# Summing the second conditioning product beside the mixers, in plain fp32

## The reference

```
cond = silu(c)                                   # c is one row of 1024
for l in range(2):
    mod = cond @ w_ada[l] + b_ada[l]             # w_ada[l]: 1024 x 6144
    sh1, sc1, g1, sh2, sc2, g2 = split(mod, 6)
    h = rms_norm(x, g_norm_mix[l]) * (1 + sc1) + sh1
    z = h @ w_in[l]                              # 1024 x 2884
    mix = concat(sparse_attention(z), gated_recurrence(z), spatial_gating(z)) @ w_out[l]
    x = x + g1 * mix
    h = rms_norm(x, g_norm_ffn[l]) * (1 + sc2) + sh2
    y = swiglu(h) if l == 0 else mixture_of_8_experts(h)
    x = x + g2 * y
x = rms_norm(x, g_final)
```

## Time and profile before

| | us |
|---|---|
| median of 3 runs | 2792.98 (2789.38 to 2796.92) |
| the profiled execution | 2798.46 |
| its span | 2796.6 |
| PE busy | 2393.7 |
| DVE busy | 1965.3 |
| ACT busy | 1401.6 |
| mean granted clock of TensorE | 0.897 of full |

### The profile page before, as it was taken

The page is one execution under the profiler, slowest core; times in us unless marked ns, Lnnn a source line. Parts: engine busy times, 40 slices in busy tenths (PEclk is TensorE's granted clock), DMA queues, the critical chain, the costliest instruction groups (busy, mean ns, idle before and its releaser), DMA issues.

```text
span 2796.6 us, 31058 instructions
## 1 busy us (share of the span) xinstructions
PE 2393.7 (86%) x12719; PEld 2029.0 (73%) x12719; DVE 1965.3 (70%) x2326; ACT 1401.6 (50%) x1354; POOL 28.0 (1%) x52
## 2 busy tenths in 40 slices
PE   5836899886378799999999999998758898878898
PEld 4726699865266688888888888886647898746898
DVE  6565654476446588888888888887554787675787
ACT  5322443342423477777776777776324434365432
POOL 1000000000000000000000000000000000000000
PEclk9866999988568799999999999999867999878999
DMA  9410745563004699999999999998421455321453
GB/s 334 134 45 5 270 150 182 200 226 124 6 19 166 233 355 357 354 355 354 356 345 348 357 354 356 355 356 307 124 75 55 147 184 195 97 76 55 145 187 106
DMA packets 293717, 590.70 MB, mean 211 GB/s; under 512 B 11702, under 2 KB 86564, under 8 KB 292928
## 3 DMA queue, kind: packets, MB, share of 16 engines
q1 hardware_dynamic: 289872, 572.33, 58.0%
q0 software_dynamic: 3696, 16.32, 1.9%
HBM read 587.56 MB, written 1.05 MB: 210 GB/s over the span
## 4 chain that ended last, share of the span: by engine, by line
PE 59%; DVE 4%; ACT 2%; DMA 1%; issue 1%; DVEq 0%; POOL 0%; SPq 0%; ACTq 0%
PE ps L1129 18%; PE ps L1131 17%; PE ps L1130 17%; PE ps L1213 1%; PE ps L1337 1%; PE ps L1198 1%; PE ps L1320 1%; PE ps L1298 1%; ACT arena L892 1%; DVE arena L1815 1%; PE ps L1236 1%; DVE arena L1650 1%; DVE xT_lo L1682 0%; DVE w_lo L1635 0%; PE ps L1187 0%
## 5 line engine op out<-in xcount | busy, mean ns | idle before, releaser
L792 ACT ACTIVATE w_hi<-raw 128x2048 fp32r<-128x2048 f32 x548 | 1041.9, 1907 | 610.5 <-PE ps L1131 486.0
L1635 DVE TENSOR_TENSOR w_lo<-raw,w_hi 128x2048 fp32r<-128x2048 f32 x548 | 1224.8, 2273 | 56.1 <-ACT w_hi L792 37.1
L1129 PE MATMUL ps<-w_hi,xT_hi 128*128 128x512 f32 (+3 forms) x1600 | 641.6, 401 | 56.3 <-DVE xT_lo L1749 25.3
L1130 PE MATMUL ps<-w_lo,xT_hi 128*128 128x512 f32 (+3 forms) x1600 | 627.7, 392 | 0.0
L1131 PE MATMUL ps<-w_hi,xT_lo 128*128 128x512 f32 (+3 forms) x1600 | 627.3, 392 | 0.0
L1129 PEld LDWEIGHTS ps<-w_hi,xT_hi 128*128 128x128 f32 x1600 | 310.1, 194 | 124.7 <-DVE xT_lo L1749 26.6
L1130 PEld LDWEIGHTS ps<-w_lo,xT_hi 128*128 128x128 f32 x1600 | 310.4, 194 | 62.6 <-issue 3.4
L1131 PEld LDWEIGHTS ps<-w_hi,xT_lo 128*128 128x128 f32 x1600 | 309.6, 194 | 63.2
L1129 PE MATMUL ps<-xT_hi,w_hi 128*128 128x256 f32 x1056 | 302.4, 286 | 6.0 <-DVE xT_lo L1682 6.0
L1130 PE MATMUL ps<-xT_lo,w_hi 128*128 128x256 f32 x1056 | 301.8, 286 | 0.0
L1131 PE MATMUL ps<-xT_hi,w_lo 128*128 128x256 f32 x1056 | 301.7, 286 | 0.0
(11 more groups left out here) (324 smaller groups left out, 1916.3 us busy)
## 6 DMA issues: line engine op xcount, KB each, us to landing
raw<-in_moe_w_gate SPq DMA_DIRECT2D x112, 1024.0 KB, 5.5
raw<-in_moe_w_up SPq DMA_DIRECT2D x112, 1024.0 KB, 5.3
raw<-in_moe_w_down SPq DMA_DIRECT2D x112, 1024.0 KB, 5.4
raw<-in_w_ada SPq DMA_DIRECT2D x48, 1024.0 KB, 5.3
raw<-in_f_w_up SPq DMA_DIRECT2D x44, 1024.0 KB, 5.0
raw<-in_f_w_down SPq DMA_DIRECT2D x22, 1024.0 KB, 4.9
raw<-in_w_in SPq DMA_DIRECT2D x20, 1024.0 KB, 5.1
raw<-in_a_w_in SPq DMA_DIRECT2D x12, 1024.0 KB, 5.4
```

The lines of the kernel that those rows point to most:

```text
L792: act.activation(w_hi[:, k % HI, 0:LEN[k]], raw[:, r, 0:LEN[k]], ACT.Copy).then_inc(w_hi_ready, 1)
L1129: pe.matmul(out_, lh, rh, start=start, stop=False)
L1130: pe.matmul(out_, lh, rl, start=False, stop=False)
L1635: dve.tensor_tensor(w_lo[:, k % RAW, 0:LEN[k]], raw[:, k % RAW, 0:LEN[k]], w_hi[:, k % HI, 0:LEN[k]].bitcast(F32), ALU.subtract).then_inc( ...
```

## The change

- `ada{l}1` moves in `ORDER` ahead of `out{l}`, and its 12 slots (`WHOLE`) are not split: ACT and DVE skip them, and PE multiplies them as loaded in plain fp32 with a stationary fp32 vector `cond_wide` (`whole`, new). The 12 slots are used in four places of PE's mixer program: slots 0 to 2 ahead of the transposes of the heads, 3 to 7 after the index scores, 8 and 9 ahead of the recurrence, 10 and 11 after its output. They use PSUM banks 4 to 7; ACT copies the six sums out (`whole_sums`, new).
- The bias of this half goes to its own place (`bias_late`); bias and sums are added between the two groups of `out{l}` (shift and scale) and after the norm rows (gate).
- In `ada{l}0` the squares, the root and the norm rows are computed between groups 2 and 3 and after group 3, beside the two gate groups, and the transposed rows go to banks 4 to 7.
- The angles of both position sets are computed in `in0`, after groups 1 and 3. At the start the vector `c` and the identity are loaded first, then the bias, `x`, the gain, and the other constants.
- The first two slots of `out{l}` are split during the two root waits of the mixer's end. `h_LF` moves from `arena` to `mix`.
- The norm gains of the second half, of `g_final` and of `kv_norm` are released (and so loaded) right after the preceding norm's rows; the root is taken ahead of the wait for the gain.

```diff
-        h_LF = Cut(arena)(768, b=2)
+        h_LF = mix[:, :, 0:BD]
+        bias_late = arena[:, 8448:8448 + 3 * D]
-        ORDER = ["ada00", "in0", "out0", "ada01", "ffn0", "ada10", "in1", "out1", "ada11", "over", "moe",
+        ORDER = ["ada00", "in0", "ada01", "out0", "ffn0", "ada10", "in1", "ada11", "out1", "over", "moe",
+        WHOLE = [BASE[name] + i for name in ("ada01", "ada11") for i in range(len(SL[name]))]
+        WHOLE_BANKS = [4, 5, 6, 7, 4, 4]
...
 # POOL
-            load(const[:, :], consts, ld_const)
+            load(cond_rows, a["c"][0].rearrange("(k p) -> k p", p=P), ld_cond)
+            load(ident, consts[:, C_ID:C_ID + P], ld_ident)
+            load(arena[:, 0:3 * D], a["b_ada"][0, 0:3 * D].partition_broadcast(P), ld_mod)
             load(X[:, :, :], a["x"][0].rearrange("(b p) n -> p b n", p=P), ld_x)
-            load(cond_rows, a["c"][0].rearrange("(k p) -> k p", p=P), ld_first)
+            load(gain, a["g_norm_mix"][0].partition_broadcast(P), ld_gain)
+            load(const[:, P:C_END], consts[:, P:C_END], ld_const)
...
 # ACT
+            def conditioned(name):
+                upto(BASE[name] + 6)
+                square_sums(X)
+                upto(BASE[name] + 7)
+                root(rstd)
+                linear(name)
+                to_columns(bank=4)
+            def whole_sums(l, groups):
+                for g in groups:
+                    act.wait_ge(w_used, BASE[f"ada{l}1"] + 2 * g + 2)
+                    dst = gate_sums[:, 512 * g - 2048:512 * g - 1536] if g >= 4 else arena[:, 512 * g:512 * g + 512]
+                    act.activation(dst, ps[:, WHOLE_BANKS[g], :], ACT.Copy).then_inc(ada_sums, 1)
...
+                upto(BASE[f"out{l}"])
                 act.wait_ge(o_out, got(o_out))
...
+                whole_sums(l, [5])
+                upto(BASE[f"out{l}"] + 1)
                 root(stat_b[:, 0:2])
                 to_columns(3)
                 linear(f"out{l}")
-                cond_columns()
-                linear(f"ada{l}1")
...
 # PE
+            def whole(l, slots):
+                for i in slots:
+                    k = n[0]
+                    pe.wait_ge(raw_full[k % RAW], 16 * (k // RAW + 1))
+                    n[0] += 1
+                    for c in range(4):
+                        last = pe.matmul(ps[:, WHOLE_BANKS[i // 2], :], cond_wide[:, i % 2 * 4 + c, :],
+                                         raw[:, k % RAW, c * FG:(c + 1) * FG], start=i % 2 == 0 and c == 0,
+                                         stop=i % 2 == 1 and c == 3)
+                    last.then_inc(w_used, 1)
...
                 linear(f"in{l}")
+                pe.wait_ge(cond_wide_ready, l + 1)
+                whole(l, range(0, 3))
                 pe.wait_ge(heads_ready, got(heads_ready))
...
+                whole(l, range(3, 8))
                 pe.wait_ge(idx_taken, got(idx_taken))
+                pe.wait_ge(ada_sums, got(ada_sums, 4))
                 attend(dsa[l], att_bufs, att_T, [
...
+                whole(l, range(8, 10))
                 pe.wait_ge(rec_rows, got(rec_rows))
...
                 last.then_inc(o_out, 1)
+                pe.wait_ge(ada_sums, got(ada_sums))
+                whole(l, range(10, 12))
                 pe.wait_ge(ws_masked, got(ws_masked))
...
                 linear(f"out{l}")
-                pe.wait_ge(cond_cols, got(cond_cols))
-                linear(f"ada{l}1", 1, True)
+                got(ada_sums)
                 to_columns(H)
...
 # DVE, in ada()
+                def rows_of_norm():
+                    upto(BASE[name] + len(SL[name]) - 1)
+                    scale_with_gain()
+                    norm_rows(True)
+                between = {2: inv_rms, 3: rows_of_norm}
+                if name == "ada00":
+                    between[1] = rows_in_memory
+                linear(name, evac, between, 1)
+                to_columns(bank=4)
...
+                linear(f"in{l}", into_rows(zrows(IN_DIM)), {} if l else {1: first_angles, 3: second_angles})
...
-                inv_root(stat_a[:, 0:12], stat_a[:, 0:12], HD)
+                inv_root(stat_a[:, 0:12], stat_a[:, 0:12], HD, lambda: upto(BASE[f"out{l}"]))
...
-                inv_root(stat_b[:, 0:2], stat_b[:, 0:2], C_DIM)
+                inv_root(stat_b[:, 0:2], stat_b[:, 0:2], C_DIM, lambda: upto(BASE[f"out{l}"] + 1))
...
-                linear(f"out{l}", into_residual(True))
-                beat().then_inc(mod_free, 1)
-                dve.wait_ge(mod_free, sent(mod_free))
-                ada(f"ada{l}1")
-                norm(True)
+                def shift_and_scale():
+                    mods[0] += 16
+                    dve.wait_ge(ld_mod, mods[0])
+                    dve.wait_ge(ada_sums, 6 * l + 4)
+                    tt(arena[:, 0:2 * D], arena[:, 0:2 * D], bias_late[:, 0:2 * D], ALU.add)
+                    scale_with_gain()
+                linear(f"out{l}", into_residual(True), {0: shift_and_scale})
+                inv_rms()
+                norm_rows(True)
+                gain_taken()
+                dve.wait_ge(ada_sums, 6 * l + 6)
+                tt(mod[:, 2, :], gate_sums[:, :], bias_late[:, 2 * D:3 * D], ALU.add)
+                to_columns()
```

More of the change, by code:

```diff
@@ L336, in build @@
         xT_lo = sb("xT_lo", [P, KC, T], F32R)
+        with nc.sbuf_tensor("cond_wide", [P, KC, P], F32) as cond_wide, nc.sbuf_tensor("gate_sums", [P, D], F32) as gate_sums:
+            pass
         aT_hi = sb("aT_hi", [P, NT, T], F32R)
@@ L1659, in stt, with linear @@
                 step(dve.scalar_tensor_tensor(o, x, s, y, op0, op1))
-            def linear(name, evac, between={}):
+            def linear(name, evac, between={}, ahead=2):
                 f = gi = i = 0
@@ L1667, in linear @@
                     per = KC // nk
[L1668 removed]
+                    upto(BASE[name] + i + per - 1 + (ahead if i + per == len(slots) else 2))
                     dve.wait_ge(w_used, BASE[name] + i + per)
@@ new lines, in ada, with first_angles @@
+                if name == "ada00":
+                    between[1] = rows_in_memory
+                linear(name, evac, between, 1)
+                to_columns(bank=4)
+            def first_angles():
+                dve.wait_ge(ld_const, 16)
+                dve.wait_ge(ld_first, 32)
+                step(dve.tensor_copy(posf[:, 0:2], posi[:, 0:2]))
+                for b in range(TB):
+                    angles(posf[:, b:b + 1], const[:, C_INV1:C_INV1 + 32], 32, sin1[:, b, :], cos1[:, b, :])
+                beat().then_inc(angles_ready, 1)
+                dve.wait_ge(angles_ready, sent(angles_ready))
@@ new lines, in second_angles @@
+            def second_angles():
+                dve.wait_ge(ld_late, 32)
+                step(dve.tensor_copy(posf[:, 2:4], posi[:, 2:4]))
+                step(dve.tensor_copy(posf[0:N_CMP, 4:5], posi[0:N_CMP, 4:5]))
+                inv2 = const[:, C_INV2:C_INV2 + 8]
+                for b in range(TB):
+                    angles(posf[:, 2 + b:3 + b], inv2, 8, sin2[:, b, :], cos2[:, b, :])
+                angles(posf[0:N_CMP, 4:5], inv2[0:N_CMP, :], 8, sinc[0:N_CMP, :], cosc[0:N_CMP, :])
+                beat().then_inc(angles_ready, 1)
+                dve.wait_ge(angles_ready, sent(angles_ready))
@@ L2216, in _ @@
                     with dve.Else():
-                        for sem, total, more in ((w_lo_ready, ROUTED, MOE_SLOTS), (dve_step, made, added)):
+                        for sem, total, more in ((w_lo_ready, ROUTED - len(WHOLE), MOE_SLOTS), (dve_step, made, added)):
                             dve.wait_ge(sem, total)
```

120 lines of the change are left out of this document (58 added, 62 removed).

## The result

| | before | after |
|---|---|---|
| median of the runs, us | 2793.7 | 2696.6 |
| profiled execution, us | 2798.5 | 2694.8 |
| its span, us | 2796.6 | 2692.6 |
| PE busy, us | 2393.7 | 2402.0 |
| mean granted clock | 0.897 | 0.917 |

The account below looks back on a forecast made before the run. PE was busy 86%, with the second conditioning half back to back on it and room in the mixers, where DVE and ACT carry the chain. -80.6 + 2.5 - 14.0 - 9.0 - 7.5 = -108.6; forecast 2685 us, range 2670 to 2705.

Parts of the forecast that it names:

- The second half leaves the path: From X's last write to the last norm row, the norm follows X at once: -41.6 and -39.6, taken as -80.6.
- The slots in the mixers: Twelve streamed slots fill PE's waits in each layer's mixers, at a cost of +1.2 and +1.3, together +2.5 us.
- the splits in the root waits: End of layer 0's mixers: splitting two slots of `out` costs +0.6 and +3.1; the layer's sum took 3.4.
- The first stage: Start to `in0`: second angles moved away and norm beside the gate groups; `in0` at about 68.4 instead of 82.39, -14.0.
- Two of the prediction's signs: Checks named in advance: `in0` starting at 66 to 71 us; DVE's split between reciprocal and root wait, 2 to 4 late.
- Layer 1's first half: From the last addition to `in1`, DVE does the norm beside the stage: -9.0 us, bounds -4 and -12.
- The gains: Norms with earlier gain loads: `g_final` -2.45, `a_norm` -0.7, `kv` -4.3; together -7.5 us, bounds -4 and -9.
- half-clock streams: Rival: the mixers' streams run at half clock and the mixers wait for them; +66, 2750 us; chance 0.11.
- That the first stage and the norm give little: Rival: DVE is late beside the gate groups and loads set the pace; terms 3 and 4 at a third, 2700; chance 0.11.
- The warm clock: Rival: the streams keep the clock up through the mixers, saving 10 us a layer; 2665 us; chance 0.10.
- The slower rival: In the four streams a plain fp32 slot costs more, eating the gain from 9.0 us; at 11, 2838; chance 0.02.

Follow-up runs that it names:

- sums_on_path: Changed kernel with the new unsplit fp32 sums kept, but all twelve slots moved back behind the output product; 2754.9 us, ratio 0.9866.
- first_loads_old: Changed kernel with GpSimd's first loads in their old order and PE's first transpose waiting for all constants; 2690.0 us.
- angles_back: Changed kernel with the second angles put back between groups 3 and 4 of the first conditioning stage, their sines ahead of the rotary ones; 2699.4 us.
- norm_after: Changed kernel with the norm of the first halves put behind the last conditioning group again, new load order kept; 2703.1 us.
- warm_gap: Changed kernel with ACT's root one split later, output slots split earlier, and six useless products before the recurrence's first level; 2669.2 us, ratio 0.9542.
- both: Changed kernel with ACT's root behind the ninth slot's split and two output slots split in DVE's wait for the output product; 2685.3 us, ratio 0.9599.
- gains_late: Changed kernel with the gain row's releases put back where they were and the gain awaited ahead of the root; 2697.4 us.

## Why the prediction was right, and where its steps were off

1. *The second half leaves the path*: right in mechanism and in size, -41.6 and -39.6 to a tenth. It held because both ends of the stretch were read from the timelines and the order of instructions between them was known. `sums_on_path` shows that the place is what paid, about 69 of 82 us (less the 3.7 named there).
2. *The slots in the mixers*, +2.5: measured +3.0, and the table's +0.9 and +2.1 are smaller than the clock's own spread in the levels (layer 1's levels 27.3 before, 30.4 after). By parts, layer 0: the first three slots +0.35 (forecast +0.4); the clock behind them -2.0 (-2.5); slots 8 and 9 -0.2 (+1.9: they ran at full clock, 3.6 us each); the warm start of the recurrence -1.6 (-2); the splits in the root waits +2.8 (+3.7, of which the prediction's sum took 3.4). These make -0.6; the measured +0.9 has besides +0.4 in `in0` itself, +0.7 in the levels and +0.4 in the stage of `out0`. In layer 1 the levels alone give +3.1, and all the rest -1.0. So that the total agrees is luck: the errors cancel, and the largest item is the levels' clock, which the forecast did not have. What I had not seen is that DVE's wait for the output product, 7 us, would have held both splits free of charge.
3. *The first stage*, -14.0: mis-sized, it gave -10.7. That the early vector `c` ends nothing earlier was right (`first_loads_old`). The second angles are 6.1 of it (`angles_back`), as I had it. The overlap of the norm gave 3.4 (`norm_after`), where 8 were left for it; 1.2 are neither's and were not taken apart. The step that failed is "After the change the last slot is split by ACT at 53.6 and by DVE at 55.9". ACT ended it at 54.8 and DVE at 59.17, 3.3 us late, and this is the whole miss: behind it the rows (6.4 us), the additions with the split (3.7) and the columns (2.5) took what was forecast. I followed the slots and the rows on DVE, and not the norm's own work in ACT's program. The squares stand ahead of the split of the eighth slot, and DVE waits 1.74 us there; the root stands ahead of the split of the ninth, and DVE waits 2.17. Moving the root gave back 1.8; moving the squares was not tried. Two of the prediction's signs: `in0` at 71.69 is just outside its 66 to 71, DVE's split in the root wait came 2.8 late, inside its 2 to 4.
4. *Layer 1's first half*, -9.0: gave -6.8. DVE waits 2.17 us for the ninth slot here too (at 523.88), and moving the root gets 1.4 to 1.6 of the 2.2 back.
5. *The gains*, -7.5: -7.9, from -2.45, -1.1 and -4.3. `a_norm` came 0.4 better than forecast, since its load landed sooner behind its release: 4.2 us, against the 4.55 of the earlier trace rows.

Of the rivals, half-clock streams did not come: every stream but the last ran at full clock, each at most 0.70 us behind work of PE at full clock; the last one began at half, as the output product ahead of it ended. That the first stage and the norm give little is out as well: they gave 17.5 of 23.0 us, where that rival left 7.7. The warm clock was right for the neighbours of a stream and wrong for the whole: the levels kept their slow start, since a gap of 3.2 us stood between the stream and them. `warm_gap` comes near that rival's 2665 by filling just that gap, but it stands on `both`, which gave 6.5 of its 23 us. The slower rival is out: a slot costs 3.49 us, and its bound was 9.0.

## What to carry to other kernels

- A stage that leaves the path is worth the distance between its two ends, read from the timelines; what it costs where it goes must be read for each wait it fills. When two engines split work for a third, follow the order of both programs through a moved wait: a root that waits for VectorE, ahead of a split that VectorE waits for, costs both.
- Before a burst of short products that is on the path, look at the idle gap ahead of it and at the clock of its first rows. Here six products of no use were worth 16 us beside `both`, more than twice what `both` gave by moving splits and roots.
- When single times of a program spread over 10 us, judge small edits by the distance between milestones, not by medians, and start the distance at an event that the edit leaves alone: from the start of the profile the same edit seemed to give 3.1 us once and 1.7 once, from the second addition 1.8 both times.

## What the runs showed of the hardware

- The granted clock can stay at half while PE is busy all the time: in `gains_late` PE was busy 24.00 of 24 us in the levels at 0.64, and its 64-column and 128-column products took 2.88 and 2.93 us a group for five groups and more before they took 1.60. The gap came ahead of it, and the length of the slow stretch differed between executions, up to three levels.
- It can also fall while PE issues without a gap: in after, the recurrence's output products of 64 columns went from 0.39 us at 233.13 to 0.64 at 233.90, back to back. PE's waits just ahead were 0.50 us at 229.98 and 1.49 at 232.41, both shorter than the 3.20 ahead of the levels; `warm_gap` has the same fall at 228.49, with the levels at full clock:

```profile
233.13 0.39 PE L1507 MATMUL ps<-Z,arena 128*128 128x64 f32 x2
233.35 0.39 PE L1508 MATMUL ps<-Z,arena 128*128 128x64 f32 x2
233.57 0.53 PE L1509 MATMUL ps<-Z,arena 128*128 128x64 f32 x2
233.90 0.64 PE L1507 MATMUL ps<-Z,arena 128*128 128x64 f32 x2
```

- Weight loads of 1 MB arrive 2.7 us apart at the start in both orders of the small loads that were tried: an order that lets PE begin 7.8 us earlier ended the stage no earlier.
- Not settled: what decides, from one execution to the next, how many levels run slow, and the 1 to 3 us by which stages behind the experts differ between executions of the same code.
